# A chunked RWKV scan on one Trainium2 core: chunks in groups of four, with block-diagonal matrices of 128 rows

## The reference, cut to what matters

```python
def step(state, inp):
    r_t, w_t, k_t, v_t, kk_t, a_t = inp
    sa = jnp.einsum('bhvk,bhk->bhv', state, -kk_t)
    state = (state * w_t[:, :, None, :] + sa[..., None] * (kk_t * a_t)[:, :, None, :]
             + v_t[..., None] * k_t[:, :, None, :])
    return state, jnp.einsum('bhvk,bhk->bhv', state, r_t)
_, out = lax.scan(step, zeros, xs)          # 512 steps
# then a norm per head, a bonus term and a gate
```

## Time and profile before

| what | value |
|---|---|
| median of three runs | 2892.34 us |
| the profiled execution, its time and its span | 2896.05 us, 2894.3 us |
| PE busy | 2724.8 us (94%) |
| DVE, ACT, POOL busy | 1523.4, 1038.9, 313.3 us |
| granted TensorE clock over the span | 0.941 |
| PE's share of the chain that ended last | 63% |
| projection, last tiles | up to 1243 us |
| scan: first and last matmul | 1247.4 and 1462.7 us |
| output projection starts | 1509.3 us |

### The profile page before, as it was taken

The page is one execution under the profiler, slowest core; times in us unless marked ns, Lnnn a source line. Parts: engine busy times, 40 slices in busy tenths (PEclk is TensorE's granted clock), DMA queues, the critical chain, the costliest instruction groups (busy, mean ns, idle before and its releaser), DMA issues.

```text
span 2894.3 us, 36453 instructions
## 1 busy us (share of the span) xinstructions
PE 2724.8 (94%) x14774; PEld 2179.9 (75%) x14774; DVE 1523.4 (53%) x2489; ACT 1038.9 (36%) x1815; POOL 313.3 (11%) x220
## 2 busy tenths in 40 slices
PE   7999999999999999989879999989899899899998
PEld 6778888999998867756547777766766578688886
DVE  3786644554445464743345778453753453533444
ACT  3465444442223342233343223243332332422322
POOL 0043310012221100000002222020000000100001
PEclk9999999999999999965579999999999999999999
DMA  3211121223233423200005665332121123233332
GB/s 120 67 51 52 52 61 57 72 83 95 88 95 93 141 66 102 65 31 1 1 1 158 204 194 171 90 107 71 60 67 57 37 70 96 75 95 95 95 95 73
DMA packets 70852, 239.06 MB, mean 83 GB/s; under 512 B 12212, under 2 KB 13109, under 8 KB 70430
## 3 DMA queue, kind: packets, MB, share of 16 engines
q1 hardware_dynamic: 63054, 208.88, 23.6%
q10 hardware_dynamic: 7632, 27.86, 2.9%
HBM read 234.06 MB, written 2.64 MB: 82 GB/s over the span
## 4 chain that ended last, share of the span: by engine, by line
PE 63%; DVE 11%; ACT 4%; issue 3%; POOL 1%; ACTq 0%; DVEq 0%; POOLq 0%
PE ps L574 50%; DVE wl L365 2%; PE ps L2654 1%; ACT wh L359 1%; PE ps L1731 1%; PE ps L1720 1%; PE ps L1704 1%; PE ps L3315 1%; DVE xl L655 1%; DVE arena L3008 1%; DVE arena L1033 1%; PE ps L1433 1%; PE ps L1569 0%; POOL arena L735 0%; DVE arena L3374 0%
## 5 line engine op out<-in xcount | busy, mean ns | idle before, releaser
L574 PE MATMUL ps<-xh,wh 128*128 128x512 f32 (+1 forms) x2728 | 1020.9, 388 | 36.5 <-DVE xl L680 15.1
L574 PE MATMUL ps<-xl,wh 128*128 128x512 f32 (+1 forms) x2728 | 993.5, 379 | 0.0
L574 PE MATMUL ps<-xh,wl 128*128 128x512 f32 (+1 forms) x2728 | 989.3, 377 | 0.0
L365 DVE TENSOR_TENSOR wl<-ring,wh 128x1024 fp32r<-128x1024 f32 x374 | 471.0, 1260 | 645.2 <-ACT wh L359 644.5
L359 ACT ACTIVATE wh<-ring 128x1024 fp32r<-128x1024 f32 x374 | 395.4, 1057 | 994.6 <-PE ps L574 888.6
L574 PEld LDWEIGHTS ps<-xh,wh 128*128 128x128 f32 x2728 | 503.7, 190 | 173.6 <-issue 53.8
L574 PEld LDWEIGHTS ps<-xl,wh 128*128 128x128 f32 x2728 | 502.1, 190 | 101.0 <-issue 9.9
L574 PEld LDWEIGHTS ps<-xh,wl 128*128 128x128 f32 x2728 | 502.9, 190 | 98.8
L735 POOL TENSOR_TENSOR arena<-arena 128x512 f32<-128x512 f32 (+1 forms) x42 | 72.0, 1721 | 1837.3 <-ACT arena L719 1837.3
L1950 PE MATMUL ps<-xh,wh 128*128 128x264 f32 (+1 forms) x816 | 258.9, 317 | 9.6 <-DVE xl L424 9.6
L1950 PE MATMUL ps<-xl,wh 128*128 128x264 f32 (+1 forms) x816 | 233.7, 286 | 0.0
(11 more groups left out here) (384 smaller groups left out, 2900.5 us busy)
## 6 DMA issues: line engine op xcount, KB each, us to landing
ring<-in_weights SPq DMA_DIRECT2D x374, 512.0 KB, 3.6
arena<-in_w_ada ACTq DMA_DIRECT2D x48, 512.0 KB, 4.6
arena<-in_cmp_w SPq DMA_DIRECT2D x2, 2048.0 KB
h<-in_x ACTq DMA_DIRECT2D x4, 528.0 KB, 6.3
arena<-strip_scratch SPq DMA_DIRECT2D x8, 264.0 KB, 3.7
out_features<-arena SPq DMA_DIRECT2D x8, 256.0 KB, 2.2
con<-in_consts SPq DMA_DIRECT2D x1, 777.0 KB, 10.8
arena<-in_c ACTq DMA_DIRECT2D x1, 512.0 KB, 4.1
```

The costliest lines, as they stand in the source:

```text
L365: dve.tensor_tensor(flat(self.wl[:, s % 2]), flat(self.ring[:, s % RING]), flat(self.wh[:, s % 2]).bitcast(F32), ALU.subtract).then_inc(se ...
L574: last = pe.matmul(self.place(u, e), w[:, k, :], x[:, k, o:o + m], start=(k == 0 and i == 0), stop=(k == self.chunks - 1 and i == 2))
```

## The change

The scan works in four groups of four chunks.

- **The state** of two heads becomes one 128 x 128 block-diagonal matrix. One matmul per pair of heads (2 per chunk, 128 rows, 128 weight columns, 128 moving columns) gives the keys' part of `x` for all four chunks of a group; only the chunk's 32 rows are read. VectorE writes states and scaled states as 64 x 64 blocks, 4 instructions instead of 2.
- **The token part of `x`**, which needs no state, is computed ahead for each group at units 21.5 to 23: 4 matmuls of 128 rows against a block-diagonal matrix `outer`, built by GpSimd; ScalarE copies the result over `MM`. VectorE's `X` is then one instruction, minus the matmul's result minus this part.
- **The output**: 2 matmuls per chunk for the state's part (128 rows, 32 moving columns) and, once per group, 8 matmuls of 128 rows against `outer` and `inner`, again filled by GpSimd. ScalarE copies once per group.
- `TT` times `X` (4 matmuls) and the state's products (8 matmuls) are as before, per chunk.
- **The plan**: `SCAN_STEP` 1.45 becomes 0.93, `widths` become 0.32, 0.48, 0.64, 0.8. The layout of `AR` changes from (pair, chunk, kind, token) to (pair, kind, chunk, token).

Cut to its core:

```diff
-SCAN_STEP = 1.45
+SCAN_STEP = 0.93
@@ RwkvScan.pool (new)
+        yield self.early - 2
+        pool.wait_ge(self.rwkv.kept.sem, self.rwkv.kept.at(12))
+        pool.wait_ge(self.rwkv.masked.sem, self.rwkv.masked.at(4))
+        pool.memset(self.outer.rearrange("p a b -> p (a b)"), 0.0).then_inc(self.cleared.sem, 1)
+        pool.wait_ge(self.cleared.sem, self.cleared.at(1))
+        for g in range(4):
+            yield self.early - 1 + 0.5 * g
+            if g:
+                pool.wait_ge(self.value_x.sem, self.value_x.at(g))
+            fill(self.outer, self.part(g, 1, 0)).then_inc(self.value_blocks.sem, 1)
...
+            fill(self.outer, self.part(g, 1, 1))
+            fill(self.inner, self.part(g, 0, 1)).then_inc(self.blocks.sem, 1)
@@ RwkvScan.tensor
+        for g in range(4):
+            yield self.early + 0.5 * g
...
+            pe.wait_ge(self.value_blocks.sem, self.value_blocks.at(g + 1))
+            for lo, t, o, r in heads:
+                last = pe.matmul(core.ps[:, g % 2, 64 * r:64 * r + 64], self.outer[:, r], self.TOK[2][:, g, o:o + 64], start=True, stop=True)
+            last.then_inc(self.value_x.sem, 1)
...
-            x_first(c)
-            for h, (lo, t, o, r) in enumerate(heads):
-                last = pe.matmul(x_bank(c, h, t), AR[lo:lo + 64, t, c, 0], STATE[lo:lo + 64, c % 2, t], start=False, stop=(t == 1))
+            for t in range(2):
+                last = pe.matmul(core.ps[:, 4, 0:256].rearrange("p (a t n) -> p t a n", a=2, t=2)[:, t],
+                                 AR[:, t, 0, 4 * g:4 * g + 4].rearrange("p c t -> p (c t)"),
+                                 STATE[:, c % 2, t].rearrange("p (a n) -> p a n", a=2), start=True, stop=True)
...
+            for t in range(2):
+                pe.matmul(core.ps[:, 5, t * P + CH * (c % 4):t * P + CH * (c % 4) + CH], STATE[:, c % 2, t], AR[:, t, 1, c],
+                          start=(c == 4 * g and t == 0), stop=False)
+            if c < 4 * g + 3:
+                continue
             yield t0 + 0.6 * d
-            out(c)
+            pe.wait_ge(self.blocks.sem, self.blocks.at(g + 1))
+            for F, M in ((lambda o, r: self.TOK[2][:, g, o:o + 64], self.outer), (lambda o, r: U[:, 64 * r:64 * r + 64], self.inner)):
+                for lo, t, o, r in heads:
+                    last = pe.matmul(core.ps[lo:lo + 64, 5, t * P:(t + 1) * P], F(o, r), M[:, r], start=False,
+                                     stop=(M is self.inner and t == 1))
@@ RwkvScan.vector
-            for e in range(2):
-                ins = dve.tensor_scalar(self.X[rows(c), 128 * e:128 * e + 128], core.ps[rows(c), 4 + e, 256 * e:256 * e + 128], -1.0, None,
-                                        ALU.mult)
-            ins.then_inc(self.x_kept.sem, 1)
+            dve.scalar_tensor_tensor(out=four(self.X[rows(c)]), in0=four(core.ps[rows(c), 4, 0:256]), scalar=-1.0,
+                                     in1=self.value_part(c // 4)[rows(c)], op0=ALU.mult, op1=ALU.subtract).then_inc(self.x_kept.sem, 1)
@@ second_block
-    widths = (0.5, 0.75, 1.0, 1.25)
+    widths = (0.32, 0.48, 0.64, 0.8)
```

More of the change, by code:

```diff
@@ L1410, in when, with part, value_part, pool @@
     def when(self, c):
         return self.at + self.step * c
+    def part(self, g, e, f):
+        return self.MM[:, g].rearrange("p (h e f t) -> p h e f t", h=4, e=2, f=2)[:, :, e, f]
+    def value_part(self, g):
+        return self.MM[:, g].rearrange("p (h e f t) -> p h e f t", h=4, e=2, f=2)[:, :, :, 0]
+    def pool(self, pool):
+        def fill(dst, src):
+            for c in range(4):
+                rows = slice(CH * c, CH * c + CH)
+                last = pool.tensor_copy(dst[rows, :, rows], src[rows])
+            return last
+        yield self.early - 2
[8 more added lines that the diff above has]
+            fill(self.outer, self.part(g, 1, 0)).then_inc(self.value_blocks.sem, 1)
+        yield self.at - 0.4
+        pool.wait_ge(self.proj.free.sem, self.proj.free.at(N2))
+        pool.memset(self.inner.rearrange("p a b -> p (a b)"), 0.0).then_inc(self.cleared.sem, 1)
+        pool.wait_ge(self.cleared.sem, self.cleared.at(2))
+        pool.wait_ge(self.value_x.sem, self.value_x.at(4))
+        for g in range(4):
+            yield self.when(4 * g)
+            if g:
+                pool.wait_ge(self.o_ready.sem, self.o_ready.at(g))
+            fill(self.outer, self.part(g, 1, 1))
+            fill(self.inner, self.part(g, 0, 1)).then_inc(self.blocks.sem, 1)
@@ L1423, in tensor @@
-        tok = lambda c: [a[rows(c), c // 4] for a in self.TOK]
-        def x_first(c):
-            for h, (lo, t, o, r) in enumerate(heads):
[L1427 to L1434, removed]
@@ L1436, in out @@
-        def out(c):
-            for lo, t, o, r in heads:
[L1438 to L1443, removed]
+        for g in range(4):
+            yield self.early + 0.5 * g
+            if g == 0:
+                pe.wait_ge(self.cmp.shifted.sem, self.cmp.shifted.at(1))
+            if g >= 2:
+                pe.wait_ge(self.value_kept.sem, self.value_kept.at(g - 1))
+            pe.wait_ge(self.value_blocks.sem, self.value_blocks.at(g + 1))
+            for lo, t, o, r in heads:
+                last = pe.matmul(core.ps[:, g % 2, 64 * r:64 * r + 64], self.outer[:, r], self.TOK[2][:, g, o:o + 64], start=True, stop=True)
+            last.then_inc(self.value_x.sem, 1)
@@ L1461, in tensor @@
             for lo, t, o, r in heads:
-                last = pe.matmul(u_bank(c, r), self.TT[rows(c), c // 4, r], X[rows(c), 64 * r:64 * r + 64], start=True, stop=True)
+                last = pe.matmul(core.ps[rows(c), 4, 64 * r:64 * r + 64], self.TT[rows(c), g, r], X[rows(c), 64 * r:64 * r + 64],
+                                 start=True, stop=True)
             last.then_inc(self.u_ready.sem, 1)
@@ L2925, in queries_ready @@
             pe.wait_ge(cmp.shifted.sem, cmp.shifted.at(1))
+            pe.wait_ge(scan.value_kept.sem, scan.value_kept.at(4))
         if s == 24:
```

86 lines of the change are left out of this document (51 added, 35 removed).

## The result

The changed kernel took 2825.56 us, median of 4 runs (2821.69 to 2829.49), against 2894.73 us for the kernel before (4 runs, 2891.94 to 2899.01): a ratio of 0.976, 95% interval 0.9739 to 0.9781. The forecast was 2865 us: the way was right and the end lies just inside the range, but the gain was 69 us where the forecast had 27 against the median. The runs of one kernel differ by up to about 1% here, at different clocks, and a profile shows only one of them.

What follows compares the result with a forecast made beforehand. PE, mostly at 1.2 GHz, was taken to bound the scan window: 217 to 188 us (29 less), 3.3 more early, 3 more for DVE, 8 less around the scan; 31 less than the profiled 2896.05: 2865 us, range 2825 to 2893.

Steps and rivals of the forecast that it cites:

- the mean clock, taken at 0.62: Window of scan and attention: clock rises from 0.53 to 0.62 (bounds 0.53 and 0.77), 14 us less of PE's 183 us.
- the rival with the released clock: Scan window: clock released for most of it, mean 0.85, 20% idle, about 2840 us, down to 2820; chance 0.20.
- clock stays: Scan window: no clock gain, 183 us at 5 to 10% idle, 2872 to 2884 us, say 2878; chance 0.22.
- PE's saving: New matmuls: 13.8 us less in the window, 3.3 more before it, 10.5 us net, bounds 25 and nothing.
- The overlap: Attention steps in the squeezed plan: unsqueezed offsets make steps overlap; idle share, now 9.4%, taken as 10%.
- The costs of the new matmuls: PE in the window: state part of x 16.0 us, output's state part 11.5, group part 7.8; 35.3 instead of 49.1.
- Full height is dear: New full-height matmuls: all at upper bounds, no clock gain, saving shrinks to nothing, 2885 to 2895 us; chance 0.08.
- The early part: Token part of x, computed in the projection at full clock: 3.3 us more, bounds 2 and 6.
- Hidden: POOL's fills between groups in the projection: 1 us and hand-overs, covered by 2.8 us until PE comes to them.
- the four state writes: DVE, each chunk's chain: 0.56 us longer, costing nothing behind attention pieces, 9 us uncovered; 3 us charged for queueing, bounds 0 and 9.
- DVE hand-overs uncovered: PE's waits for X and U: 40 us instead of 7 if every chunk paid both, about 2911 us, slower; chance 0.10.
- Behind the scan: Stretch after the scan, and its start: two steps move to better places, 8 us less of the 16 us idle there.

Runs made afterwards that it cites:

- run 19: Not a label: "a run 19 us above its kernel's median" is the profiled run, 2854.72 us, of the kernel before with only the new plan's due times.
- experiment 9: Kernel before, its scan, step and widths untouched, only the offsets inside and between attention steps made longer by 1 / 0.64: 2837.24 us, ratio 0.9806.
- 1: Changed kernel with the due times of the kernel before (step 1.45, widths 0.5 to 1.25): 2891.16 us, ratio 0.9968.
- 6: Changed scan with the step and widths of before, but offsets inside and between attention steps longer by 1 / 0.64: 2816.66 us, ratio 0.9706.
- 4: Changed kernel with 20 small matmuls (32 rows, 32 weight columns, 64 moving columns) added per chunk, results unused: 2894.38 us, ratio 0.9974.
- 5: Changed kernel with four full-height matmuls (128 rows, 128 weight and moving columns) added per chunk, results unused: 2829.38 us, ratio 0.9754.
- 2: Kernel before with only the due times changed to the new plan (step 0.93, widths 0.32 to 0.8): 2836.17 us, ratio 0.9791.
- 7: Changed kernel with VectorE's four state writes per chunk doubled, the added ones ahead, to unused columns: 2844.85 us, ratio 0.9824.
- 10: Changed kernel with the four scalings of the old state per chunk moved from VectorE to ScalarE: 2822.46 us, ratio 0.9748.
- 3: Kernel before with four full-height matmuls (128 rows, 128 weight and moving columns) added per chunk, results unused: 2919.35 us, ratio 1.005.
- 8: Changed kernel with the plan squeezed further by 0.87 (step 0.81, widths 0.28 to 0.7): 2815.18 us, ratio 0.9714.
- 12: Changed kernel with attention offsets longer by 1 / 0.64, step 1.26, widths 0.43 to 1.09, and state scalings on ScalarE: 2806.62 us, ratio 0.97.

## Why the prediction was right and where it fell short

The runs fill a table of three plans and two scans (ratio to before, and in the profiled run idle time and clock of the scan's stretch):

| plan | old scan | new scan |
|---|---|---|
| of before | 1; 20.3 us, 0.53 | 0.9968; 34.0 us, 0.61 |
| new plan | 0.9791; 4.3 us, 0.62 | 0.976; 14.1 us, 0.84 |
| of before, long offsets | 0.9806; 3.7 us, 0.72 | 0.9706; 14.6 us, 0.91 |

The old scan's 0.62 is from a run 19 us above its kernel's median and its 0.72 from one 10 us below, so these two don't rank the plans.

**The step that failed: the mean clock, taken at 0.62.** It was 0.84. By the forecast's own formula, 62% instead of 18% of the 183 us runs fast, 183 x 0.62 x 0.44 = 50 us less instead of 14, 133 us busy; measured were 125.9. The 36 us of this term are most of the 48 us by which the scan, 140 us, came out under the forecast's 188. Some 8 us more lie in the formula: the clock is a mean over time, and the forecast used its share of time as a share of the work. At 0.84, 68% of the time is fast, and by the scores' 0.56 that is 79% of the work; counted so for both kernels, the 183 us become 125, and at the forecast's own 0.62 they would have been 161 instead of 169 (estimates from the earlier trace rows). The upper bound of 0.77 was too low as well; it was taken from a stretch in which PE is idle for a third. The idle share was right (10%, measured 14.1 of 140 us), and the rival with the released clock had 0.85 and about 2840 us. It would have been the nearer forecast; its 20% idle were too many. Two smaller sums are off: *clock stays* comes to 2870 to 2880 us with the other terms, not 2872 to 2884, and the bounds of PE's saving to 27 and 2 us, not 25 and nothing.

**Why it was mis-sized.** The forecast gave the low clock to the company of small matmuls, and so to the new scan, and gave the plan no part in it beyond idle time. In the profiles both act. Matmuls left alone and order changed: 0.53 to 0.72 (experiment 9), 0.61 to 0.91 (1 to 6). Order left alone and matmuls changed: 0.84 to 0.71 with small ones, to 0.88 with full-height ones (4, 5). The evidence that made the forecast discount the order was the earlier trace rows, a stretch at 0.50 in which PE never stops; after has its like, and a stretch at the full clock with more idle time in it:

```profile
1258.00:1270.00 12.00, 12.00 (x71) 8.79 (x68) 6.46 (x21) 3.26 (x8) 0.00 (x0) 0.51 0.00 0
...
1280.00:1328.00 48.00, 42.41 (x436) 28.84 (x434) 39.43 (x145) 26.18 (x82) 5.19 (x16) 1.00 0.01 1
```

PE is busy for 12.00 of 12 us at 0.51 and for 42.41 of 48 us at 1.00. So busy time doesn't give the clock, and the forecast was right in that; its mistake was to conclude that the order is then worth only the waits it removes. The Trainium skill, TensorE: Matmul & The Clock Gate, "Part 1: The HAM clock gate", has activity release the throttle. As busy time this is contradicted here once more; whether another measure of activity would fit both rows, the runs don't tell. What it is in the closer overlap that raises the clock, the waits between pieces, or which pieces follow each other, stays open.

**The overlap.** That in-step offsets which are not squeezed make steps overlap, and that PE then has more to do between scores and transposes, was seen, but was worth a change of the idle share from 9.4 to 10% in the sum. Alone it is worth 60 us (2, 9). It is the first cause of the whole result: without it the new scan brings 8.5 us of 69 (1).

**The costs of the new matmuls** were right for two of three. PE's timeline of after: the state part of x at the low clock, the output's state part at the full and at the low clock, and the group output at the low clock:

```profile
1258.29 1.22 PE L1475 MATMUL ps<-arena 128*128 128x128 f32 x4
1259.30 0.85 PE L1770 MATMUL ps<-con,arena 128*128 128x128 f32 x3
...
1281.58 0.63 PE L1496 MATMUL ps<-arena 128*128 128x32 f32 x4
1282.05 1.10 PE L1941 MATMUL ps<-arena,con 128*128 128x512 f32 x2
...
1395.08 1.06 PE L1496 MATMUL ps<-arena 128*128 128x32 f32 x4
1395.95 0.88 PE L1770 MATMUL ps<-con,arena 128*128 128x128 f32 x3
1396.77 1.98 PE L1504 MATMUL ps<-arena 128*64 128x128 f32 x16
1398.67 1.49 PE L1754 MATMUL ps<-arena 64*128 64x512 f32 x4
```

The state part of x took 1.01 us (forecast 1.0) and the group output 1.90 us (1.96). The output's state part took 0.87 us at the low clock, where 0.7 was forecast with an upper bound of 1.04, and 0.47 us at the full one. The rule of the Trainium skill in TensorEngine Tiling (Array Packing), "When to Use Tiling", that short contractions should be cut into row tiles, is not borne out at these sizes: 128 more full-height instructions cost some 4 us by the medians (5), 640 more small ones 69 us (4), 0.03 against 0.11 us each, what they do to the clock included. *Full height is dear*, which had every part at its upper bound and no gain in clock, is refuted.

**What the new scan is worth.** In the same offsets it is a ratio of 0.9706 for 0.9806; with the new plan, or the old, 0.3 percentage points, 9 us, and with the new plan no difference that the intervals tell apart. The profiles of 9 and 6, which share their plan, show where a part of it goes: the scan is 153.9 us in the one and 132.7 in the other, but starts at 1243.8 and at 1250.4, and the output projection starts at 1435.0 and 1423.0 us. Of 21 us less in the scan, 12 are left.

**The early part** cost more than its 3.3 us. The scan starts 10.9 us later. With the same plan the new scan alone delays the projection's end by 6.2 to 7.0 us (1248.0 for 1241.8 us in experiment 1 and before, 1245.6 for 1238.65 in 6 and 9), and the squeezed plan adds 2 to 4, the attention's steps that move into the projection. The gap from the projection's last matmul to the scan's first grows too, from 5.6 to 7.9 us. POOL is part of it. PE's timeline and POOL's:

```profile
1216.39 1.00 PE L1466 MATMUL ps<-arena 128*128 128x64 f32 x8
1217.22 0.50 PE L1280 MATMUL ps<-con,arena 128*128 128x128 f32 x3
...
1221.68 1.08 PE L1466 MATMUL ps<-arena 128*128 128x64 f32 x8 [1.19 <-POOL arena L1427]
```
```profile
1212.58 1.28 POOL L1427 COPY arena<-arena 32x128 f32<-32x128 f32 x4 [65.27 <-PE ps L1466]
1217.45 4.08 POOL L1427 COPY arena<-arena 32x128 f32<-32x128 f32 x4 [3.60 <-PE ps L1466]
```

A group of value matmuls is 0.83 us from its start to the next piece (0.67 in the rows, 0.83 with what was added for the change of operands): 3.3 us, as forecast. A copy takes 287 ns, within the forecast 0.2 to 0.3 us, and a fill 1.28 us. But one fill took 4.08 us, and PE waited 1.19 us for it, with the projection queued behind. "Hidden" was wrong, by 1.2 us, and PE waiting for POOL was one of the two signs named as wrong at once; the other, weights of 128 columns above 0.26 us, did not come. Some 2 us of the delay were there before the first of these matmuls; their cause stays open.

**DVE.** `X` took 419 ns (forecast 450), and the rates of the other instructions were as in the earlier trace rows. That the four state writes cost nothing behind pieces of attention was wrong: 1.13 us more of them per chunk, 18 us in all, cost 19 us (7), so nothing covered them. At that rate the 0.56 us that the change adds per chunk would be some 9 us; that is an extrapolation, no run made the writes shorter. What the forecast overlooked is that the price comes by way of the clock too. The two more scalings are free (10). *DVE hand-overs uncovered* did not come: PE waited 3.6 us in all for `X` and 1.8 us for `U`, not 40.

**Behind the scan** 10.0 us went, with 8 forecast for both ends. That was luck: the forecast counted idle time, and of it only 2.1 us went (12.3 for 14.4 us). The other 7.9 are busy time, 139 instructions for 162 at a clock of 0.83 for 0.76. **The signs named ahead**: the output projection starts at 1434.9 (forecast 1480), the scan's last matmul at 1398.3 (1435); the mean clock of the stretch told the cases apart at once, as said.

## What to carry to other kernels

When a merged order is planned by hand and squeezed, look at what is not squeezed with it: here constants inside a step decided how many steps overlap, and lengthening them alone brought 60 us with the old scan (9), where the rewritten part alone brought 8.5 (1). Test plan and code apart, each with the other left as it was, before crediting either. And where TensorE runs below its full clock, a new order can return more than the waits it removes (61 us for 17 us of waits in 9), and small matmuls added can cost more than their length (69 us for 39 at the full clock in 4): give the clock that the new order may bring a scenario of its own with real weight.

## What the runs showed of the hardware that was not expected

- The scan's stretch, with 1586 matmul instructions of the same code in both, ran at a mean clock of 0.53 or 0.72 by the order alone, 195.0 or 150.2 us busy (before, 9).
- 640 small matmul instructions (32 rows, 32 weight columns, 64 moving columns) took the clock from 0.84 to 0.71; 128 of full height raised it to 0.88 (4, 5). In the old scan they raised it from 0.53 to 0.61 in the profiled run, while the median over the whole span hardly moved (3).
- The clock is not the same in each execution of one kernel, and the time follows it: the kernel before ranged from 2888.92 us at a mean of 0.943 to 2919.06 us at 0.932 in its 25 runs, experiment 9 from 2824.91 at 0.963 to 2847.12 at 0.952. An order that changes the clock can be compared only by several runs.
- A fill of four POOL copies of 32 x 128 took 1.28 us, and once in each profile about 4.1 us (4.08 to 4.11 in after and experiments 1, 6, 8 and 12); one of its copies took 2.2 us, where the median is 0.29. DVE is then in a product of two tensors:

```profile
1214.26 1.22 DVE L365 TENSOR_TENSOR wl<-ring,wh 128x1024 fp32r<-128x1024 f32 x1
1215.39 4.10 DVE L1380 TENSOR_TENSOR arena<-arena 128x2048 f32<-128x2048 f32 x1
```

  It lasts from 1215.39 to 1219.49 us, and POOL's copy began at 1217.45. The Trainium skill, GPSIMD Engine Reference, "1. Specifications", says that POOL's interfaces to SBUF are shared with VectorE and contend with its instructions that have two inputs there. The rows agree, with 2.8 us for one fill; no run took the product away.
